# Attention in which the scores are made once, and transposed after the exponential

## The chip, the core and the metric

The kernel runs on one core of a Trainium2 chip. TensorE (PE in the rows; PEld is its weight load) multiplies matrices into the eight PSUM banks of 512 float32 columns; VectorE (DVE), ScalarE (ACT) and GpSimd (POOL) do the rest, and SyncE (SP) issues the large transfers. Each engine takes its own list of instructions in order, and they wait for one another by semaphores. The metric is the time of the program on the device in microseconds (us), median of several runs.

## The reference

One decoder layer over 1024 tokens of width 1024. The part that matters here is the attention of 8 query heads in 2 key/value groups (head size 64), with three branches whose outputs are weighed by gates:

```python
s_c = einsum(q, k_cmp) - slope * d_c;  p_c = masked_softmax(s_c, d_c >= 0)      # 63 compressed keys
s_s = einsum(q, ks) - slope * d_s;     p_s = masked_softmax(s_s, d_s >= 0)      # selected blocks
s_w = einsum(q, kw) - slope * d_w;     p_w = masked_softmax(s_w, window of 512) # sliding window
o   = g0 * p_c @ v_cmp + g1 * p_s @ vs + g2 * p_w @ vw
```

With 16 blocks and a top-k of 16 the selected branch sees every earlier key, so it is plain causal attention over 1024 tokens. Around the attention stand a projection (23 units of 128 columns), a convolution branch, an output projection and a gated feed-forward of width 2816.

## The kernel before

Everything is laid out with channels on the partitions. A float32 operand of a matmul is split into a high and a low part, and products are made of two or three of these parts. The large products (`unit_tile`, L309 to L319) run in 97 units; they are not touched.

The attention stands between unit 22 and unit 23 and is a loop over the two groups `g`. In each group the query tiles `i` are 0 to 7 (128 queries of each of 4 heads), and key tiles `j` are of 128 keys. Per group it goes in these stages:

1. Copies and splits of keys and queries (ScalarE L520 to L548, VectorE L718 to L743), and the compressed keys (PE L964, L973).
2. The first scores, queries on the partitions: 32 rows (head, query tile), each of two units of up to two PSUM banks. PE makes them (`scores`, L982 and L983, masks L996), VectorE takes the negated maximum of each branch (L747) into `nmax`. PE may be two rows ahead.
3. `nmax` is turned on PE (L1033), split (L552, L764) and taken by two DMAs into rows of the query operand `QB`; the values are turned too (L1040, L555, L766).
4. The second scores, keys on the partitions, in 74 steps (`STEPS`, one key tile of one branch of one query tile, 4 heads side by side in 512 columns). The maximum comes in through the extra rows of `QB` and `KB`, so that the exponential can be taken directly: PE L1059, L1060 and a mask L1063; ScalarE takes the exponential twice from PSUM, rounded (L565, into `PTH`) and in full (L566, into `EB`); VectorE subtracts (L799, into `PTL`); PE multiplies by the values (L1078 to L1080). The scores of step s+3 are made ahead of the values of step s, in four PSUM banks.
5. At the end of each query tile the three outputs `OT` are copied from PSUM (VectorE L805 twice, ScalarE L572 once), turned on PE (L1089), divided and weighed on VectorE (L780, L784, L791), summed on POOL (L440, L442), and squared on ScalarE (L576).

The order of all this is written out by hand; the waits say how far one engine may be ahead of another.

## Time and profile before

| | us |
|---|---|
| Three runs | 1532.84, 1532.97, 1534.7 |
| Span of the profiled execution | 1532.4 |
| PE busy | 1453.2 |
| DVE busy | 707.4 |
| ACT busy | 457.7 |
| Attention, 297 to 673 us of the span | 376 |

The profiled execution is told by its span alone; the runs' median lies 0.6 us above it. In the page a busy time is the time in which at least one instruction of the engine was under way, and "mean ns of one" the duration of one, which for matmuls and ScalarE instructions overlaps with the next one. The distance from start to start of two instructions in the timeline is what one of them costs in a row of them.

### The profile page before, as it was taken

How to read it: one execution, taken by the hardware profiler on the slowest of the kernel's cores; microseconds unless marked ns; L12 is line 12 of the kernel's file. 1: busy time of each engine (PE TensorE's matmuls, PEld its weight loads, DVE VectorE, ACT ScalarE, POOL GpSimd, SP SyncE). 2: the span in 40 equal slices, each digit the busy share in tenths (PEclk: the TensorE clock that was granted, in tenths of full speed). 3: DMA queues.
4: the chain of work that ended last, by engine and by line, in shares of the span. 5: the costliest groups of instructions: out<-in, count | busy, mean ns of one | idle time of the engine just before them, and what ended most of it. 6: DMA issues, size and time to landing. Idle time of an engine off the chain costs nothing.

```text
span 1532.4 us, 17433 instructions
## 1 busy us (share of the span) xinstructions
PE 1453.2 (95%) x6670; PEld 1153.6 (75%) x6670; DVE 707.4 (46%) x871; ACT 457.7 (30%) x638; POOL 62.5 (4%) x56
## 2 busy tenths in 40 slices
PE   3999999999898998989989999999999999999995
PEld 2888888876565765668868888888888888888874
DVE  6422331186565866654353434343443524344356
ACT  5221222323677236842123211212111121211211
POOL 1100000000211002110020000000000000000000
PEclk9999999799998999999989999999999999999997
DMA  5211111000000030011101111111111011111102
GB/s 185 68 41 41 55 55 68 8 1 3 1 1 7 1 112 1 1 56 55 55 14 55 44 53 41 55 55 41 55 41 55 32 64 41 55 41 41 55 1 109
DMA packets 18690, 67.65 MB, mean 44 GB/s; under 512 B 2088, under 2 KB 2856, under 8 KB 18472
## 3 DMA queue, kind: packets, MB, share of 16 engines
q1 hardware_dynamic: 18396, 66.03, 12.2%
q0 software_dynamic: 240, 0.93, 0.3%
q8 instruction: 31, 0.51, 0.1%
q14 instruction: 23, 0.19, 0.0%
HBM read 63.01 MB, written 4.19 MB: 44 GB/s over the span
## 4 chain that ended last, share of the span: by engine, by line
PE 88%; DVE 5%; issue 2%; ACT 2%; POOL 1%; DMA 1%; DVEq 0%; SPq 0%; ACTq 0%; POOLq 0%
PE PS L314 18%; PE PS L315 18%; PE PS L318 18%; PE PS L1156 5%; PE PS L1160 5%; PE PS L1157 5%; PE PS L982 3%; PE PS L983 2%; PE PS L1078 2%; PE PS L1079 2%; PE PS L1080 2%; PE PS L1059 1%; PE PS L1060 1%; DVE nmax L747 1%; PE PS L964 1%
## 5 line engine op out<-in xcount | busy, mean ns | idle before, releaser
L314 PE MATMUL PS<-R,wh 128*128 128x512 f32 x1200 | 471.1, 393 | 9.5 <-DVE R L285 7.6
L315 PE MATMUL PS<-R,wh 128*128 128x512 f32 x1200 | 470.0, 392 | 0.0
L318 PE MATMUL PS<-R,wl 128*128 128x512 f32 x1200 | 371.8, 391 | 0.0
L314 PEld LDWEIGHTS PS<-R,wh 128*128 128x128 f32 x1200 | 227.3, 189 | 59.9 <-issue 12.6
L315 PEld LDWEIGHTS PS<-R,wh 128*128 128x128 f32 x1200 | 227.2, 189 | 47.5 <-issue 0.2
L318 PEld LDWEIGHTS PS<-R,wl 128*128 128x128 f32 x1200 | 227.1, 189 | 47.4
L299 ACT ACTIVATE wh<-raw 128x1024 fp32r<-128x1024 f32 x97 | 101.7, 1049 | 176.5 <-PE PS L1160 174.0
L882 DVE TENSOR_TENSOR F<-PS,F 128x1024 f32<-128x1024 f32 x88 | 107.6, 1223 | 92.1 <-PE PS L1160 92.1
L306 DVE TENSOR_TENSOR wl<-raw,wh 128x1024 fp32r<-128x1024 f32 x97 | 120.0, 1245 | 62.9 <-ACT wh L299 62.2
L1156 PE MATMUL PS<-R,wh 128*128 128x512 f32 x352 | 137.1, 389 | 1.1 <-DVE wl L306 1.1
L1157 PE MATMUL PS<-R,wh 128*128 128x512 f32 x352 | 136.9, 389 | 0.0
L799 DVE TENSOR_TENSOR wl<-raw,wh 128x512 fp32r<-128x512 f32 x148 | 102.7, 696 | 61.3 <-ACT raw L566 59.4
L862 DVE SCALAR_TENSOR_TENSOR F<-PS,params,F 128x1023 f32<-128x1023 f32 x22 | 28.2, 1283 | 180.6 <-ACT F L617 180.6
L1160 PE MATMUL PS<-R,wl 128*128 128x512 f32 x352 | 108.4, 389 | 0.0
L747 DVE TENSOR_REDUCE nmax<-PS 128x1 f32<-128x64 f32 (+4 forms) x192 | 91.3, 537 | 16.7 <-PE PS L996 15.7
L565 ACT ACTIVATE wh<-PS 128x512 fp32r<-128x512 f32 x148 | 91.4, 617 | 21.0 <-PE PS L1063 12.5
L566 ACT ACTIVATE raw<-PS 128x512 f32<-128x512 f32 x148 | 91.9, 621 | 0.0
L982 PE MATMUL PS<-R 128*128 128x512 f32 (+4 forms) x208 | 86.6, 417 | 2.6 <-DVE R L742 1.8
L617 ACT ACTIVATE F<-PS,params 128x1024 f32<-128x1024 f32 x22 | 26.6, 1208 | 192.5 <-PE PS L318 192.5
L1078 PE MATMUL PS<-wh,R 128*65 128x512 f32 x148 | 68.1, 460 | 12.6 <-DVE wl L799 6.0
L870 DVE TENSOR_TENSOR F<-F,PS 128x1024 f32<-128x1024 f32 x22 | 26.9, 1221 | 115.0 <-PE PS L318 114.9
L983 PE MATMUL PS<-R 74*128 74x512 f32 (+4 forms) x208 | 79.0, 386 | 0.0
(138 smaller groups left out, 1376.2 us busy)
## 6 DMA issues: line engine op xcount, KB each, us to landing
raw<-in_w_units SPq DMA_DIRECT2D x97, 512.0 KB, 3.2
F<-in_xT SPq DMA_DIRECT2D x16, 512.0 KB, 7.5
outT<-F SPq DMA_DIRECT2D x8, 512.0 KB, 3.0
F<-in_w_cmp SPq DMA_DIRECT2D x1, 2048.0 KB, 7.7
masks<-in_masks POOLq DMA_DIRECT2D x1, 448.0 KB, 5.6
R<-in_alibi_q POOLq DMA_DIRECT2D x2, 160.0 KB, 5.3
R<-R SPq DMA_DIRECT2D x4, 48.0 KB
R<-in_alibi_k POOLq DMA_DIRECT2D x1, 136.0 KB, 3.4
```

The source lines that it names most:

```text
L306: nc.vector.tensor_tensor(wl[:, slot, :], raw[:, slot, :], f32(wh[:, slot, :]), ALU.subtract)\
L314: nc.tensor.matmul(out, w_h, hi(kt)[:, cols], start=first, stop=False)
L315: nc.tensor.matmul(out, w_h, lo(kt)[:, cols], start=False, stop=False)
L318: last = nc.tensor.matmul(out, w_l, hi(kt)[:, cols], start=False, stop=end)
L747: return nc.vector.tensor_reduce(nmax[:, br, i, h:h + 1], pair(2 * (b % 2) + unit)[:, col:col + count], AX.X, ALU.max, negate=True)
L799: nc.vector.tensor_tensor(PTL[s % 4], EB[s % 4], f32(PTH[s % 4]), ALU.subtract).then_inc(pt_lo, 1)
L882: nc.vector.tensor_tensor(x1, pair(DOWN_PAIRS[d]), x1, ALU.add).then_inc(down_added, 1)
L982: nc.tensor.matmul(out, QA[:, i, h, :], KA[:, key:key + count], start=True, stop=False)
L983: nc.tensor.matmul(out, QB[0:DH + AR, i, h, :], KB[0:DH + AR, key:key + count], start=False, stop=not masked)
L1156: nc.tensor.matmul(out, w_h, act_at(par_pair, a, 0)[:, cols], start=a == 0, stop=False)
L1157: nc.tensor.matmul(out, w_h, act_at(par_pair, a, 1)[:, cols], start=False, stop=False)
L1160: last = nc.tensor.matmul(out, w_l, act_at(par_pair, a, 0)[:, cols], start=False, stop=a == 1)
```

## The change

The two kinds of scores become one. A phase is now (group, query tile, part), part 0 for the selected branch and part 1 for the window, 32 phases in all; the compressed branch is attached to one of the two parts (`CMP_IN_A`). A phase has four rows, one for each head, and its steps are the key tiles of its branches, 148 over both groups.

For a row PE makes the scores with queries on the partitions, VectorE takes the maximum, and ScalarE takes the exponential with the maximum as bias into SBUF (`EA`, `EB`). For a step PE turns four 128x128 blocks of these exponentials (`turn_weights`) into one PSUM bank, ScalarE copies them rounded into `PTH`, VectorE subtracts from PSUM into `PTL`, and PE multiplies by the values two steps later. The rows of a phase are put among the steps of the phase before it (`step_of_row`). The row scores, the turned outputs and the turned values share two pairs of PSUM banks (`SLOTS`). All the `OT` copies are now ScalarE's. The compressed keys and values of both groups are made ahead of the loop. The DMAs of the maxima are gone. SyncE loads units 24 to 26 before the attention, and the residual input x after it.

```diff
+PHASES = [(g, i, part) for g in range(KV) for i in range(TT) for part in range(2)]
+STEPS = [(p, i, br, j) for p, (g, i, part) in enumerate(PHASES) for br, j in key_tiles(i, part)]
+def step_of_row(r):
+    p, h = divmod(r, GROUP)
+    if p == 0:
+        return -1
+    if p == len(PHASES) // KV:
+        return FIRST_STEP[p] - 1
+    return FIRST_STEP[p - 1] + h * (FIRST_STEP[p] - FIRST_STEP[p - 1]) // GROUP
+ROWS_AT = [[r for r in range(NROWS) if step_of_row(r) == s] for s in range(-1, len(STEPS))]
...
@@ sync
-                for part, src, done in ((0, MH, mt_hi), (1, ML, mt_lo)):
-                    sp.dma_start(f32(QB[row:row + 3, :, :, :])..., f32(src[0:96, :])).then_inc(m_in, 16)
...
+            sp.wait_ge(t_ready, KV * NS)
+            sp.wait_ge(pt_lo, KV * NS)
+            for k in range(KT):
+                sp.dma_start(F1[:, X1 + k, :], xT[k]).then_inc(x1_in, 16)
@@ scalar
-                        act.wait_ge(st_ready, NS * g + s + 1)
-                        nc.scalar.activation(PTH[s % 4], PS[:, s % 4, :], ACT.Exp).then_inc(pt_hi, 1)
-                        nc.scalar.activation(EB[s % 4], PS[:, s % 4, :], ACT.Exp).then_inc(e_ready, 1)
+            def exponentials(r):
+                act.wait_ge(max_ready, r + 1)
+                last = nc.scalar.activation(weights[:, 0:wide], scores[:, 0:wide], ACT.Exp, bias=nmax[:, r, 0:1])
+                if with_cmp:
+                    last = nc.scalar.activation(weights[:, wide:wide + CW], scores[:, wide:wide + CW], ACT.Exp,
+                                                bias=nmax[:, r, 1:2])
+                last.then_inc(e_ready, 1)
...
+            for s in range(KV * NS + 2):
+                    act.wait_ge(t_ready, s + 1)
+                    if s > 3:
+                        act.wait_ge(pv_done, s - 3)
+                    nc.scalar.activation(PTH[s % 4][0:tall, :], PS[0:tall, 4 + s % 2, :], ACT.Copy).then_inc(pt_hi, 1)
+                    ...
+                        nc.scalar.activation(OT[STEPS[ENDS[b] - 1][2]], PS[0:DH + 1, 6 + b % 2, :], ACT.Copy)
+                    for r in ROWS_AT[s + 1]:
+                        exponentials(r)
+                    ...
@@ vector
+            for s in range(KV * NS + 1):
+                    dve.wait_ge(pt_hi, s + 1)
+                    nc.vector.tensor_tensor(PTL[s % 4][0:tall, :], PS[0:tall, 4 + s % 2, :], f32(PTH[s % 4][0:tall, :]),
+                                            ALU.subtract).then_inc(pt_lo, 1)
+                    ...
+                for t in range(TURNS):
+                    if step_of_turn(t) == s:
+                        weigh(t)
+                    for r in ROWS_AT[s + 1]:
+                        maxima(r)
@@ tensor
-                    for c in range(0, width, BANK):
-                        scores(bank + c // BANK, 0, h, i, key + c, min(BANK, KEYS - key - c), ...)
-                def key_scores(s):
-                    ...
+                for c in range(0, wide, BANK):
+                    scores(c, key + c, min(BANK, wide - c), c == 0 and diag >= BANK and not edge)
+            def turn_weights(s):
+                if s == FIRST_STEP[p]:
+                    pe.wait_ge(e_ready, GROUP * (p + 1))
+                if s > 1:
+                    pe.wait_ge(pt_lo, s - 1)
+                for h in range(GROUP):
+                    last = nc.tensor.transpose(PS[0:tall, 4 + s % 2, h * P:(h + 1) * P],
+                                               weights_of(h, part)[:, col:col + tall], ident)
+                last.then_inc(t_ready, 1)
...
+            for s in range(KV * NS):
+                turn_weights(s)
+                ...
+                for r in ROWS_AT[s + 1]:
+                    row_scores(r)
+                ...
+                    for v in values_at(s):
+                        values(v)
             order = [4, 5, 6, 7, 0, 1, 2, 3]
-            for n in (OUT0, OUT0 + 1):
-                unit_matmuls(pe, n, 0, 0, 0, n % 3, m_hi, m_lo, order, order[:4])
+            unit_matmuls(pe, OUT0, 0, 0, 0, OUT0 % 3, m_hi, m_lo, order, order[:4])
+            turn(TURNS - 1)
+            pe.wait_ge(o_scaled, TURNS)
+            unit_matmuls(pe, OUT0 + 1, 0, 0, 0, (OUT0 + 1) % 3, m_hi, m_lo, order, order[:4])
```

On ScalarE, in the steps of a group of the kernel before: L565 and L566 are the two exponentials of a step, L576 the squares.

```order
L565 ACTIVATE wh<-PS 128x512 [waits pv_done,st_ready]
L566 ACTIVATE raw<-PS 128x512
L562 REGISTER_ALU
L565 ACTIVATE wh<-PS 128x512 [waits pv_done,st_ready]
L566 ACTIVATE raw<-PS 128x512
L575 REGISTER_ALU
```

ScalarE in the changed kernel, in the phase of query tile 6, window part: L632 is the copy into `PTH`, L650 the copy of an output, L611 the exponential of a row of the next phase.

```order
L632 ACTIVATE wh<-PS 128x512 [waits pv_done,t_ready]
L650 ACTIVATE PBm<-PS 65x512 [waits ot_turned,pv_done]
L611 ACTIVATE F1<-PS,nmax 128x896 [waits max_ready]
L613 ACTIVATE F1<-PS,nmax 128x64
L632 ACTIVATE wh<-PS 128x512 [waits pv_done,t_ready]
L611 ACTIVATE F1<-PS,nmax 128x896 [waits max_ready]
L613 ACTIVATE F1<-PS,nmax 128x64
L632 ACTIVATE wh<-PS 128x512 [waits pv_done,t_ready]
```

Before, each ScalarE instruction of a step waited for PE alone. Now a copy, which VectorE waits for, stands behind an exponential, which itself waits for VectorE.

VectorE before, in the steps: L799 is the subtraction, L805 a copy of an output.

```order
L805 COPY PBm<-PS 65x512 [waits pv_done]
L798 REGISTER_ALU
L799 TENSOR_TENSOR wl<-raw,wh 128x512 [waits e_ready]
L798 REGISTER_ALU
L799 TENSOR_TENSOR wl<-raw,wh 128x512 [waits e_ready]
L780 RECIPROCAL coef<-PS 128x12 [waits ot_turned]
```

VectorE in the changed kernel: L882 is the subtraction, L850 and L852 the maxima of a row of the next phase.

```order
L882 TENSOR_TENSOR wl<-PS,wh 128x512 [waits pt_hi]
L850 TENSOR_REDUCE nmax<-PS 128x1 [waits s_ready]
L852 TENSOR_REDUCE nmax<-PS 128x1
L882 TENSOR_TENSOR wl<-PS,wh 128x512 [waits pt_hi]
L850 TENSOR_REDUCE nmax<-PS 128x1 [waits s_ready]
L852 TENSOR_REDUCE nmax<-PS 128x1
```

The maxima, which had a stage of their own in which VectorE did little else, now stand each behind the subtraction of a step.

PE in the changed kernel, in a window phase: L1143 turns exponentials, L1111, L1112 and L1118 make a row, L1156 to L1158 multiply by the values.

```order
L1143 MATMUL PS<-consts,F 128x128 [waits pt_lo]
L1143 MATMUL PS<-consts,F 128x128 x3
L1111 MATMUL PS<-R 128x512 [waits e_ready]
L1112 MATMUL PS<-R 128x512
L1111 MATMUL PS<-R 128x128
L1112 MATMUL PS<-R 128x128
L1111 MATMUL PS<-R 128x64
L1112 MATMUL PS<-R 128x64
L1118 MATMUL PS<-masks 128x128 x2
L1118 MATMUL PS<-masks 128x64
L1156 MATMUL PS<-wh,R 65x512 [waits pt_lo]
L1157 MATMUL PS<-wh,R 65x512
```

A row waits for the exponential of the row two before it, so PE can be ahead of the other two by a step, not more.

## Rows read from the trace of the kernel before

**Rows 1.** The page: span, busy us (share) xinstructions, GB/s in 40 slices.
```profile
span 1532.4 us, 17433 instructions
PE 1453.2 (95%) x6670; PEld 1153.6 (75%) x6670; DVE 707.4 (46%) x871; ACT 457.7 (30%) x638; POOL 62.5 (4%) x56
...
GB/s 185 68 41 41 55 55 68 8 1 3 1 1 7 1 112 1 1 56 55 55 14 55 44 53 41 55 55 41 55 41 55 32 64 41 55 41 41 55 1 109
```

**Rows 2.** Windows: length, busy us of PE, PEld, DVE, ACT, POOL; PE clock, DMA.
```profile
297.00:307.00 10.00, 8.71 (x41) 8.36 (x41) 5.39 (x8) 2.49 (x5) 0.00 (x0) 0.50 0.00 0
307.00:363.00 56.00, 55.60 (x325) 41.91 (x326) 47.94 (x100) 8.94 (x9) 0.00 (x0) 0.96 0.00 1
...
561.00:673.00 112.00, 103.11 (x496) 65.11 (x497) 68.58 (x114) 82.92 (x173) 16.95 (x15) 0.99 0.12 45
sum 376.00, PE 346.19 PEld 239.85 DVE 250.09 ACT 200.27 POOL 35.50; mean PE 43.27 PEld 29.98 DVE 31.26 ACT 25.03 POOL 4.44
```

**Rows 3.** Timeline of the steps: start, us, engine, line, operation.
```profile
428.87 0.65 ACT L566 ACTIVATE raw<-PS 128x512 f32<-128x512 f32 x1
429.34 0.66 ACT L565 ACTIVATE wh<-PS 128x512 fp32r<-128x512 f32 x1
429.55 0.69 DVE L799 TENSOR_TENSOR wl<-raw,wh 128x512 fp32r<-128x512 f32 x1 [0.28 <-ACT raw L566]
```

**Rows 4.** Groups by form, DVE, 280 to 760 us: busy us, mean ns, idle before.
```profile
L799 DVE TENSOR_TENSOR wl<-raw,wh 128x512 fp32r<-128x512 f32 x148 | 102.7, 696 | 61.3 <-ACT raw L566 59.4
L747 DVE TENSOR_REDUCE nmax<-PS 128x1 f32<-128x640 f32 x40 | 31.9, 813 | 0.0
L791 DVE TENSOR_TENSOR F<-PS,coef 128x768 f32<-128x768 f32 x16 | 15.2, 949 | 0.1
L747 DVE TENSOR_REDUCE nmax<-PS 128x1 f32<-128x64 f32 x64 | 14.0, 219 | 16.6 <-PE PS L996 15.7
L732 DVE SCALAR_TENSOR_TENSOR R<-F,R 64x512 fp32r<-64x512 f32 x16 | 10.8, 683 | 0.3
L747 DVE TENSOR_REDUCE nmax<-PS 128x1 f32<-128x1024 f32 x8 | 9.7, 1213 | 0.0
L747 DVE TENSOR_REDUCE nmax<-PS 128x1 f32<-128x128 f32 x16 | 3.8, 278 | 0.0
```

**Rows 5.** Groups by form, ACT, 280 to 760 us.
```profile
L565 ACT ACTIVATE wh<-PS 128x512 fp32r<-128x512 f32 x148 | 91.4, 617 | 21.0 <-PE PS L1063 12.5 <-PE PS L1060 7.9
L576 ACT ACTIVATE F<-F 128x256 f32 x14 | 5.8, 418 | 32.7 <-POOL F L442 32.7
L590 ACT ACTIVATE R<-PS,params 128x1024 fp32r<-128x1024 f32 x4 | 4.3, 1113 | 12.2 <-PE PS L1117 12.2
L526 ACT ACTIVATE hidc<-PS,posb 128x63 f32<-128x63 f32 x4 | 1.3, 314 | 12.1 <-PE PS L964 12.1
```

**Rows 6.** Timeline of PE: the gates' transposes, and two score matmuls in a row.
```profile
286.80 1.03 PE L942 MATMUL PS<-consts,F 128*128 128x128 f32 x8
320.23 0.40 PE L983 MATMUL PS<-R 74*128 74x512 f32 x1
320.47 0.40 PE L982 MATMUL PS<-R 128*128 128x512 f32 x1
```

**Rows 7.** Windows of 1 us inside the steps of the first group.
```profile
392.00:393.00 1.00, 0.48 (x2) 0.33 (x3) 0.86 (x3) 1.00 (x3) 0.00 (x0) 1.00 0.00 0
399.00:400.00 1.00, 0.00 (x0) 0.00 (x0) 0.03 (x1) 1.00 (x3) 0.00 (x0) 1.00 0.00 0
401.00:402.00 1.00, 1.00 (x4) 0.71 (x3) 0.84 (x2) 1.00 (x3) 0.00 (x0) 0.50 0.00 0
```

**Rows 8.** Timeline: ScalarE's first copy for the attention; the ends of the attention.
```profile
289.73 1.06 ACT L520 ACTIVATE raw<-F 64x1024 f32 x1
...
668.57 0.39 PE L1080 MATMUL PS<-wl,R 128*65 128x512 f32 x1
...
684.86 0.46 PE PS L318 x2
```

More of the change, by code:

```diff
@@ new lines, in values_turned @@
+                    .then_inc(v_hi, 1)
+            act.wait_ge(qkv_ready, N_QKV)
+            for g in range(KV):
+                to_compress(CK[:, g, :], g, 0, ck_ready)
+            for half in range(2):
+                keys(0, half)
+            for g in range(KV):
+                to_compress(CV[g], g, 1, cv_ready)
+            act.wait_ge(hidk_ready, 1)
+            act.wait_ge(posb_ready, 1)
+            nc.scalar.activation(hidc[:, 0:2, :], PS[:, 6, 0:2 * NCMP].rearrange("p (g n) -> p g n", g=KV),
+                                 ACT.Gelu_apprx_tanh, bias=posb[:, 0:1]).then_inc(geluk_ready, 1)
@@ L809, in _ @@
-                steps.leave()
+            for half in range(2):
+                keys(0, half)
+            dve.wait_ge(kcp_ready, 1)
+            nc.vector.tensor_copy(kcmp[:, :, :], PS[0:DH, 7, 0:2 * NCMP].rearrange("p (g n) -> p g n", g=KV))\
+                .then_inc(kcmp_ready, 1)
+            dve.wait_ge(vcp_ready, 1)
+            nc.vector.tensor_copy(vcmp[:, :, :], PS[0:NCMP, 6, 2 * P:2 * P + KV * DH].rearrange("p (g d) -> p g d", g=KV))\
+                .then_inc(vcmp_ready, 1)
+            for h in range(GROUP):
+                queries(0, 0, h)
@@ new lines, in _, with maxima @@
+            keys_compressed(0)
+            values_turned(0)
+            def maxima(r):
+                p, h = divmod(r, GROUP)
+                g, i, part = PHASES[p]
+                dve.wait_ge(s_ready, r + 1)
+                scores = pair(slot("row", r))
+                wide = P * (i + 1 if part == 0 else min(i, WT) + 1)
+                with_cmp = CMP_IN_A[i] == (part == 0)
+                last = nc.vector.tensor_reduce(nmax[:, r, 0:1], scores[:, 0:wide], AX.X, ALU.max, negate=True)
+                if with_cmp:
+                    last = nc.vector.tensor_reduce(nmax[:, r, 1:2], scores[:, wide:wide + CW], AX.X, ALU.max, negate=True)
+                last.then_inc(max_ready, 1)
@@ new lines, in _ @@
+            last.then_inc(vt_ready, 1)
+            for g in range(KV):
+                pe.wait_ge(cv_ready, 2 * g + 2)
+                for l in range(CMP_BLOCK // 2):
+                    last = nc.tensor.matmul(PS[:, 4 + g, 0:NCMP], W1C[:, 1, l, :],
+                                            CV[g][:, 2 * l:2 * l + CMP_STRIDE * (NCMP - 1) + 1:CMP_STRIDE],
+                                            start=l == 0, stop=l == CMP_BLOCK // 2 - 1)
+                last.then_inc(hidv_ready, 1)
+            pe.wait_ge(geluk_ready, 1)
@@ new lines, in _ @@
+            pe.wait_ge(posb_ready, 1)
+            nc.tensor.matmul(PS[0:DH, 7, 0:KV * NCMP], w2c[:, 0, :], hidc[:, 0:2, :].rearrange("p g n -> p (g n)"),
+                             start=True, stop=True).then_inc(kcp_ready, 1)
+            pe.wait_ge(geluv_ready, 2)
+            for g in range(KV):
+                last = nc.tensor.matmul(PS[0:NCMP, 6, 2 * P + g * DH:2 * P + (g + 1) * DH], hidc[:, 2 + g, :], w2c[:, 1, :],
+                                        start=True, stop=True)
+            last.then_inc(vcp_ready, 1)
@@ new lines, in values @@
+            def values(s):
+                p, i, br, j = STEPS[s]
+                tall = CW if br == CMP else P
+                pe.wait_ge(pt_lo, s + 1)
+                first, end = s == 0 or s in ENDS, s + 1 in ENDS
+                b = sum(e <= s for e in ENDS)
+                if first and b > 1:
+                    pe.wait_ge(ot_copied, b - 1)
+                n, out = (0, TT, 2 * TT)[br] + j, PS[0:DH + 1, 6 + b % 2, :]
+                nc.tensor.matmul(out, VH[0:tall, n, 0:DH + 1], PTH[s % 4][0:tall, :], start=first, stop=False)
+                nc.tensor.matmul(out, VL[0:tall, n, 0:DH + 1], PTH[s % 4][0:tall, :], start=False, stop=False)
+                nc.tensor.matmul(out, VH[0:tall, n, 0:DH + 1], PTL[s % 4][0:tall, :], start=False, stop=end).then_inc(pv_done, 1)
```

606 lines of the change are left out of this document (291 added, 315 removed).

## Prediction

> **What bounds the kernel now.** I read the page first: PE is busy 95% of a span of 1532.4 us, no other engine half of it [rows 1]. So an edit that only takes work from PE ought to pay. Then the windows, to find the attention: it lies between 297 and 673 us, 376 us, of which PE is busy 346; the first scores of a group take 56 us, its steps 112, and the rest is preparation [rows 2]. Third the timeline in the steps: ScalarE starts an exponential every 0.47 us, though each is told as 0.65, and VectorE starts 0.03 us after the second of them ends, 428.87 + 0.65 = 429.52 against 429.55 [rows 3]. That is what a hand-over between two engines costs there. Last the groups by form, for the price of every operation that the change keeps in another order [rows 4, 5]. What I look for is whether PE stays the bound when the other two engines are made to wait for each other.
>
> **What PE gets rid of.** Two score matmuls of 512 columns start 0.24 us apart [rows 6]. The second scores, 148 x 2 of these and 56 masks, go: about 352 x 0.235 = 83 us less. The first scores lose the columns beyond the diagonal, which every row of a 512-bank carried: some 20 us. Four transposes for each of 148 steps come: eight take 1.03 us [rows 6], of which the last one's tail is 0.27 (one alone is a 128-column matmul), so 0.11 to 0.13 each, 592 of them 65 to 77 us. That price was seen at the full clock; it is the nearest row to the new ones, which read the same float32 form from SBUF. In the new loop PE's own work is transposes 68, values 148 x 3 x 0.235 = 104, rows 84 and their masks 17, turned outputs 14: about 285 us. The maxima's DMAs and their waits go too, and one set-up of the second group.
>
> **What the new order makes ScalarE and VectorE do.** In each of 103 of the 148 steps at least one row of the next phase is worked on (88 with one, 12 with two, 3 with four; one more set of four comes ahead of the first step). In such a step the order rows show a closed round: ScalarE's copy; VectorE's subtraction, which waits for it; VectorE's maximum, queued behind the subtraction; ScalarE's exponential, which waits for the maximum; and the next step's copy, queued behind the exponential. Nothing in this round can overlap with the rest, however far ahead PE is. Its pieces:
>
> - Copy 0.60 (between the 0.617 mean and the undisturbed ones) and subtraction 0.69 [rows 4, 5]; three hand-overs of 0.03 to 0.05 [rows 3]; off it go 0.12 that a ScalarE instruction starts ahead of the other's told end, and 0.06 for VectorE's: 1.23 us, x 103 = 126.7 us. That the subtraction now reads PSUM where it read SBUF is not in a row of that size; between nothing more and 0.1 us each (10 us), I take nothing, since the 768-column L791 reads PSUM in 0.949, which is 0.69 scaled up.
> - The maxima: they have the very lengths of before, 128 wide ones and 64 of 64 columns. From 0.278 at 128 over 0.813 at 640 to 1.213 at 1024, 0.16 for a small one that follows [rows 4]: 98 us without the first phase.
> - The exponentials with a bias: the nearest rows with a per-partition operand from PSUM are 0.314 at 63 columns and 1.113 at 1024 [rows 5], a straight line of 0.26 + 0.00083 per column. 128 wide ones with 67,584 columns in all give 89, the 64 small ones 0.19 each 12: 100 us without the first phase. Without the bias' share it would be 90, and by L565's own rate of 0.617 for 512 some 95.
> - Where a step has two or four rows, maximum and exponential of neighbours do overlap: 12 us off.
>
> Together 313 us. To it come, on the same path: 45 steps without a row at VectorE's pace of 0.65 (29 us); 15 times the weighing, three dependent VectorE instructions of which the largest is 0.949, 1.5 us in all, and the squares at 0.45 of ScalarE, in the same queues (29 us); 12 splits of queries at 0.683, less their overlap, and the keys of the second group (12 us); 14 starts of phases of up to four steps, where the transposes must wait for the exponential just made, 0.5 us each (7 us). That is 390 us. The last phase, which has no rows and runs at PE's 1.16 us a step, adds 3; the change of group, where the last values are multiplied, copied, and the new values split before a maximum may start, 5; the output copies of ScalarE, which wait for values queued on PE behind two rows, 4. The loop then is 402 us, against PE's 285 in it: PE stands still for 30% of it, and no longer sets the time.
>
> **Before and after the loop.** ScalarE is free at 289.7, and its copies of 1024 columns take 1.06 us each [rows 8]. It has four of compressed keys, two of keys, four of compressed values: 300.3. PE, at half its clock there as before (0.50, rows 2), needs until about 312.5 for three sets of 16 matmuls; the queries (eight of 0.53), the values' high part (about 1.1) and the exponential's table follow, then the first four rows and transposes. I put the first copy of step 0 at 322.5, between 319 and 324. The last value matmul then is at 322.5 + 402 = 724.5, where it was at 668.6 [rows 8]: 56 us later. At the end half of unit 23 now covers the output copy, but unit 24 waits on PE for the last weighing and for VectorE's split, which stands behind the norm's first instructions; before, both halves covered these, up to 684.9 [rows 8]. I count 3 us against the change. The 4 MB of x come after the loop, on SyncE's queue ahead of unit 27; x is first needed some 29 us after the last values, and unit 27 later. At the rate of the kernel's start (185 GB/s, rows 1: 22 us) that is hidden; if it were not, some 5 us.
>
> Sum: 1532.4 + 56 + 3 = 1591.4, and with the 0.6 us between this span and the runs' median 1592.
>
> **A rule against the change.** In the first group's steps PE was busy 48% of a microsecond and kept the clock of 1.00, but after two in which it stood still the clock was 0.50, the lower of its two levels, 1.2 GHz [rows 7]. So short gaps did no harm there, a gap of 2 us did.
>
> The Trainium skill (TensorE: Matmul & The Clock Gate, section "A second HAM failure mode: psum-queue depth-cycling") tells of a kernel that cycles through PSUM banks, whose small pauses made the clock go up and down and cost throughput. By that rule the time is that of the first rival below; the trace agrees only for the longer gap.
>
> **Rivals.**
>
> 1. *The clock falls in the loop.* PE would idle some 0.5 to 1 us in each round and 2 us at starts of phases and at the change of group. At the lower clock PE's 285 us become about 525 (matmuls double, weight loads and waits don't), more than the 402 of the round, and PE sets the pace: +120 us if it were so throughout. At that pace PE is busy all the time and the clock comes back, so a third of the loop is what I would expect: +43, 1635 us. For it: the gaps. Against it: the 1.00 at 48% [rows 7]. 16%.
>
> 2. *PE stays the bound, and the change pays.* If ScalarE and VectorE do not form the round, because maxima and exponentials find room in the time in which PE multiplies, the loop takes PE's 285 us and some 10 for starts: it ends at about 618 instead of 669, less the 3 at the end: 1484 us. It decides where a step with a row takes less than PE's 1.16 + 0.8 = 2 us; the round has 1.23 + 0.81 + 0.79 = 2.8 already for 640 columns. Idle of VectorE in the steps before, 61 us behind L566 [rows 4], speaks for it: there is room on the engine, if the order let it be used. 9%.
>
>    The Trainium skill (TensorE: Matmul & The Clock Gate, section "Architectural detail: the array is 16× 32×32, not 1× 128×128") says that ScalarE and VectorE are strict FIFO while PE may pull weight loads ahead. By it the round stands, and no rival of this kind is left; the trace of before has no instruction that shows it by itself.
>
> 3. *It comes out even.* The round is shorter than counted by a sixth (exponentials at the rate without bias, ScalarE's overlap twice as large, starts hidden) and the prologue shorter: 402 + 25 becomes 345 + 22: within a few us of 1532. 4%.
>
> **How the numbers follow.** Forecast 71%, rival 1 16%, rival 2 9%, rival 3 4%. The prices in the round are off by perhaps 5% either way (16 us), the overlaps at the starts by 10; the errors that I can name (PSUM reads, PE not ahead after a turned output, cold starts) all make it longer. The forecast's own range is 1565 to 1625; with rival 1 in it the range is 1560 to 1645, and rival 2 is left out. What is within 0.2% (3 us) can't be told from no change here. Faster: rival 2 and half of rival 3, 0.11. Same: 0.01. Slower: 0.88.
>
> **What would show it.** In the changed kernel the waits should have ScalarE's exponentials waiting for VectorE's maxima, and VectorE's subtraction waiting for ScalarE's copy, each some 60 to 150 us in all, and the chain of waits should lead through these two engines in the loop, with PE busy for some 85% of the longer span instead of 95%. A step of query tile 7's rows (1024 columns) should last 3.5 us from copy to copy, one of 640 columns 2.7 to 2.8. PE should be busy 70 to 75% between 323 and 725 us, with the clock near 1.00; 0.7 there would be rival 1. Groups L747's time should be unchanged. I am wrong if a step with a row takes about 2 us (the round is not closed), if the transposes cost twice the 0.13 us (PE back as the bound, +70 on its side), or if the feed-forward after the attention changes its length, which nothing here touches.

## The result, and the profile after

| | before | after |
|---|---|---|
| median us (lowest to highest) | 1533.63 (1532.84 to 1534.7) | 1637.07 (1636.52 to 1638.9) |
| span of the profiled execution | 1532.4 | 1634.8 |
| mean granted clock of the span | 0.969 | 0.926 |
| end of the last value matmul (start: 668.57 and 768.96) | 669 | 769.4 |

After over before is 1.068 [1.0664, 1.0695]: 103 us slower. It is slower, as forecast, and within the range, but only in the part of it that the first rival had added: the forecast's own range ended at 1625. The forecast of 1592 was 45 us short, and the time is the one that the first rival had given (1635).

The page of the changed kernel, against [rows 1]: span, busy times, then the row of clocks and the chain of waits.

```profile
span 1634.8 us, 17328 instructions
...
PE 1484.8 (91%) x6970; PEld 1196.5 (73%) x6970; DVE 691.1 (42%) x839; ACT 499.8 (31%) x723; POOL 50.1 (3%) x56
...
PEclk9999999756989767999997999999999999999997
...
PE 78%; DVE 11%; ACT 6%; issue 4%; DMA 0%; POOL 0%; DVEq 0%; SPq 0%; ACTq 0%
```

Each digit of the clock row is 41 us, and the loop is the ninth to the nineteenth. Six of these are below 9, and five of the six (5 and 6, then 7, 6 and 7) lie at the starts of the two groups. In the chain VectorE and ScalarE together hold 17% of the span, 278 us.

Its waits between 320 and 790 us (who waited for whom: us in all, times, longest):

```profile
DVE wl L882 <- ACT wh L632: 205.0, 127, 4.5
ACT F L611 <- DVE nmax L852: 67.6, 41, 2.8
ACT F L611 <- DVE nmax L850: 65.8, 44, 2.9
ACT PBm L650 <- PE PS L1158: 56.4, 36, 4.9
...
PE PS L1143 <- ACT F L613: 36.4, 16, 4.0
...
ACT wh L632 <- PE PS L1143: 30.5, 45, 1.4
```

The first three rows are the closed round: VectorE's subtraction waits for ScalarE's copy, ScalarE's exponentials wait for VectorE's maxima. It is visible link by link in the timeline of the two engines at query tile 7 (start, us, engine, line):

```profile
503.31 0.59 ACT L632 ACTIVATE wh<-PS 128x512 fp32r<-128x512 f32 x1
...
503.93 0.69 DVE L882 TENSOR_TENSOR wl<-PS,wh 128x512 fp32r<-128x512 f32 x1 [1.67 <-ACT wh L632]
504.54 1.22 DVE L850 TENSOR_REDUCE nmax<-PS 128x1 f32<-128x1024 f32 x1
...
505.79 1.11 ACT L611 ACTIVATE F<-PS,nmax 128x1024 f32<-128x1024 f32 x1 [1.42 <-DVE nmax L850]
506.80 0.59 ACT L632 ACTIVATE wh<-PS 128x512 fp32r<-128x512 f32 x1
...
507.43 0.69 DVE L882 TENSOR_TENSOR wl<-PS,wh 128x512 fp32r<-128x512 f32 x1 [1.67 <-ACT wh L632]
508.03 1.22 DVE L850 TENSOR_REDUCE nmax<-PS 128x1 f32<-128x1024 f32 x1
509.28 1.11 ACT L611 ACTIVATE F<-PS,nmax 128x1024 f32<-128x1024 f32 x1 [1.89 <-DVE nmax L850]
510.30 0.59 ACT L632 ACTIVATE wh<-PS 128x512 fp32r<-128x512 f32 x1
```

Each instruction starts within 0.04 us of the told end of the one before it or ahead of it, and the next copies start at 506.80 and 510.30: 3.5 us from copy to copy, as forecast. The 24 steps with one row of 640 columns and no compressed part, forecast at 2.7 to 2.8 us, took 2.77 at the least, but 3.34 in the median. What was not priced shows in windows: length, then busy us of PE, PEld, DVE, ACT, POOL, the clock, DMA. First the whole loop, then its four quarters, then three single windows.

```profile
325.00:770.00 445.00, 357.63 (x1949) 262.71 (x1948) 222.39 (x400) 225.77 (x445) 22.38 (x31) 0.80 0.01 1
325.00:436.00 111.00, 89.01 (x441) 65.06 (x440) 49.10 (x101) 52.64 (x112) 5.81 (x8) 0.69 0.00 1
436.00:551.00 115.00, 91.35 (x537) 66.93 (x535) 65.69 (x104) 64.30 (x118) 4.93 (x7) 0.91 0.01 2
551.00:661.00 110.00, 87.51 (x446) 65.03 (x445) 49.32 (x103) 51.43 (x113) 6.63 (x10) 0.69 0.00 1
661.00:770.00 109.00, 89.77 (x533) 65.68 (x532) 58.27 (x92) 57.40 (x105) 5.01 (x7) 0.92 0.01 2
...
325.00:335.00 10.00, 7.61 (x44) 7.16 (x43) 4.25 (x12) 5.66 (x14) 0.00 (x0) 0.50 0.00 0
...
385.00:395.00 10.00, 9.53 (x32) 5.81 (x31) 4.08 (x7) 4.41 (x10) 0.00 (x0) 0.50 0.00 0
...
497.00:507.00 10.00, 8.62 (x48) 5.53 (x46) 5.35 (x7) 6.03 (x11) 0.00 (x0) 1.00 0.00 0
```

The clock was 0.80 over the loop and 0.69 in the first half of either group. At 385 to 395 us it was 0.50, the lower level (1.2 GHz), and PE was busy 9.53 of 10 us there: at that clock PE is the bound again, while VectorE and ScalarE are busy less than half the time. In the timeline of that place, all three engines (start, us, engine, line):

```profile
380.35 0.69 DVE L882 TENSOR_TENSOR wl<-PS,wh 128x512 fp32r<-128x512 f32 x1 [2.45 <-ACT wh L632]
...
382.41 0.63 PE L1158 MATMUL PS<-wl,R 128*65 128x512 f32 x1
...
382.84 1.05 PE L1143 MATMUL PS<-consts,F 128*128 128x128 f32 x4
...
383.08 0.59 ACT L650 ACTIVATE PBm<-PS 65x512 f32<-65x512 f32 x1 [2.76 <-PE PS L1158]
383.57 1.25 ACT L611 ACTIVATE F<-PS,nmax 128x512 f32<-128x512 f32 x2
...
384.71 0.59 ACT L632 ACTIVATE wh<-PS 128x512 fp32r<-128x512 f32 x1
...
385.33 0.69 DVE L882 TENSOR_TENSOR wl<-PS,wh 128x512 fp32r<-128x512 f32 x1 [2.85 <-ACT wh L632]
```

A 512-column matmul takes 0.42 to 0.44 us from start to start here (0.24 in [rows 6], at the full clock), the four transposes 1.05 (0.60 to 0.66 at the full clock). And the copy of an output (L650) has waited 2.76 us for PE, with both exponentials and the next copy queued behind it: at a low clock the round passes through PE as well. The step takes 5.0 us, from one subtraction to the next (380.35 to 385.33).

Where the excess lies is told best by the phases, each from its first copy to the next phase's. In us, group 0 (phase 2i is the selected part of query tile i, 2i+1 its window part; phases 0 to 6, of short rows, are called the narrow ones below, 7 to 14 the wide ones). The middle column was summed after the result, from the prediction's prices:

| phases | by the prediction's prices, step by step | after |
|---|---|---|
| 0 to 6 | 65 | 81.2 |
| 7 to 14 | 123 | 126.6 |
| 15 with the change of group | 15.5 | 19.9 |

Group 1 reads 82.2, 125.6 and 8.4 (its last phase has no rows). The wide phases were priced within 3%; the narrow ones, at the low clock, were short by 16 to 17 us in each group.

### The profile page after: what moved, and what is told of

The parts are those of the page before. It is cut to its first block, busy times and chain, and to the rows that moved or that the text cites. A ratio compares the mean times of both kernels' runs of the same rounds, so it can differ in the third digit from the quotient of the medians.

```text
span 1634.8 us, 17328 instructions
## 1 busy us (share of the span) xinstructions
PE 1484.8 (91%) x6970; PEld 1196.5 (73%) x6970; DVE 691.1 (42%) x839; ACT 499.8 (31%) x723; POOL 50.1 (3%) x56
## 4 chain that ended last, share of the span: by engine, by line
PE 78%; DVE 11%; ACT 6%; issue 4%; DMA 0%; POOL 0%; DVEq 0%; SPq 0%; ACTq 0%
PE PS L364 17%; PE PS L365 17%; PE PS L368 17%; PE PS L1247 5%; PE PS L1251 5%; PE PS L1248 5%; DVE wl L882 4%; DVE nmax L850 3%; PE PS L1143 3%; ACT wh L632 2%; PE PS L1111 2%; PE PS L1112 2%; ACT F L611 2%; PE PS L1156 1%; PE PS L1157 1%
## 5 line engine op out<-in xcount | busy, mean ns | idle before, releaser
L882 DVE TENSOR_TENSOR wl<-PS,wh 128x512 fp32r<-128x512 f32 (+1 forms) x148 | 101.0, 689 | 205.1 <-ACT wh L632 205.0
L1143 PE MATMUL PS<-consts,F 128*128 128x128 f32 (+1 forms) x592 | 110.0, 317 | 67.1 <-ACT F L613 36.4
L1143 PEld LDWEIGHTS PS<-consts,F 128*128 128x128 f32 (+1 forms) x592 | 82.0, 160 | 117.0 <-ACT F L613 43.8
L611 ACT ACTIVATE F<-PS,nmax 128x640 f32<-128x640 f32 (+7 forms) x128 | 88.9, 698 | 133.9 <-DVE nmax L852 67.6
L1111 PE MATMUL PS<-R 128*128 128x512 f32 (+4 forms) x256 | 103.6, 408 | 27.8 <-ACT F L613 9.1
L632 ACT ACTIVATE wh<-PS 128x512 fp32r<-128x512 f32 (+1 forms) x148 | 86.4, 593 | 30.7 <-PE PS L1143 30.5
L850 DVE TENSOR_REDUCE nmax<-PS 128x1 f32<-128x640 f32 (+7 forms) x128 | 89.5, 700 | 14.6 <-PE PS L1118 13.9
L1111 PEld LDWEIGHTS PS<-R 128*128 128x128 f32 x256 | 62.5, 244 | 38.8 <-ACT F L613 12.1
L1112 PE MATMUL PS<-R 74*128 74x512 f32 (+4 forms) x256 | 88.7, 389 | 0.0
```

The source lines that it names most:

```text
L611: last = nc.scalar.activation(weights[:, 0:wide], scores[:, 0:wide], ACT.Exp, bias=nmax[:, r, 0:1])
L850: last = nc.vector.tensor_reduce(nmax[:, r, 0:1], scores[:, 0:wide], AX.X, ALU.max, negate=True)
L882: nc.vector.tensor_tensor(PTL[s % 4][0:tall, :], PS[0:tall, 4 + s % 2, :], f32(PTH[s % 4][0:tall, :]), ALU.subtract).then_inc(pt_lo, 1)
L1111: nc.tensor.matmul(out, QA[:, i, h, :], KA[:, key:key + count], start=col % BANK == 0, stop=False)
L1112: return nc.tensor.matmul(out, QB[0:DH + AR, i, h, :], KB[0:DH + AR, key:key + count], start=False, stop=stop)
L1143: last = nc.tensor.transpose(PS[0:tall, 4 + s % 2, h * P:(h + 1) * P], weights_of(h, part)[:, col:col + tall], ident)
```

## The experiments

Ratios are against the kernel before, run on the same chip (medians there 1534.91, 1532.04, 1533.9 and 1531.22 for the four sets). "Loop" is the time from 325 us to the last value matmul of the profiled execution, 444 in the changed kernel. The expectations weigh three explanations of its length: the closed round, PE's low clock, and from set two on the queue in which ScalarE's output copies stand.

Set one asks whether the round is closed, and whether PE's amount of work matters.

**e1: VectorE takes the maxima of the coming rows ahead of the subtraction.** The round's second and third link are exchanged, so that a maximum no longer waits for ScalarE's copy; the weighing of a turned output moves with them.

```diff
             for s in range(KV * NS + 1):
                 if s < KV * NS:
+                    ... (weigh, if due)
+                    for r in ROWS_AT[s + 1]:
+                        maxima(r)
                     dve.wait_ge(pt_hi, s + 1)
                     nc.vector.tensor_tensor(PTL[s % 4] ...
-                    for r in ROWS_AT[s + 1]:
-                        maxima(r)
```

> Edit: VectorE takes the maxima of a step's rows (and weighs a turned output) before the subtraction of that step instead of behind it; everything else is the changed kernel's. Round theory (copy, subtraction, maximum, exponential, next copy each wait for the one before): the maximum no longer stands behind the subtraction, so the round is cut to copy and exponential on ScalarE beside maximum and subtraction on VectorE, about 1.3 to 1.5 us for a row of 640 columns instead of 2.8. PE's 2.0 us a step then sets the pace, the clock stays at its higher level, the loop falls from 444 us to 300 to 340 and the time to 1495 to 1535 us. Clock theory alone (the round is not what makes PE wait): PE's work and its pauses are what they were, 1620 us or more.

Measured: 1541.67 us (1540.46 to 1545.37), ratio 1.0053 [1.0032, 1.0073]; loop 350 us. In the page the subtraction's group, whose last numbers are the idle time before it, and the window of the whole loop:

```profile
L889 DVE TENSOR_TENSOR wl<-PS,wh 128x512 fp32r<-128x512 f32 (+1 forms) x148 | 101.0, 683 | 33.9 <-ACT wh L632 33.6
```

```profile
325.00:676.00 351.00, 312.50 (x1950) 233.78 (x1949) 222.95 (x400) 223.63 (x445) 22.41 (x31) 0.90 0.01 2
```

That is 7 us above the 1495 to 1535 expected of the round and far from the 1620 of the clock alone. The wait for the copy fell from 205 to 34 us, and 95 of the 103 us are back with not one operation removed: VectorE and ScalarE are as busy as before the exchange (222 and 226 against 223 and 224). That is the closed round, shown. The clock rose with it, from 0.80 to 0.90, and has a share in the 95; e2 and e6 below tell the two apart. Phases 7 to 14 went from 126.6 to 95.8 us and phases 0 to 6 from 81.2 to 63.9.

**e2: ScalarE's exponentials of a step stand behind the next step's copy** (except in a phase's last step). The same round, opened on the other engine.

```diff
                     nc.scalar.activation(PTH[s % 4][0:tall, :], PS[0:tall, 4 + s % 2, :], ACT.Copy)...
+                    for r in (ROWS_AT[s] if s and exp_late(s - 1) else []):
+                        exponentials(r)
...
-                    for r in ROWS_AT[s + 1]:
+                    for r in ([] if exp_late(s) else ROWS_AT[s + 1]):
                         exponentials(r)
```

> Edit: ScalarE takes the exponentials of a step's rows behind the copy of the next step instead of ahead of it, except at the last step of a phase, where the next transposes need them. VectorE's order is the changed kernel's. Round theory: the other place at which the round can be opened; inside a phase a step costs the longer of ScalarE's 1.3 and VectorE's 1.5 us for 640 columns, so PE sets the pace there, but the last step of each of 30 phases still goes the whole round. Between e1 and the changed kernel: 1510 to 1560 us. Clock theory alone: 1620 us or more.

Measured: 1577.17 (1572.07 to 1577.77), ratio 1.0277 [1.026, 1.0294]; loop 379 at a clock of 0.87. It takes back 60 us, less than the expected least. In the wide phases it is nearly as good as e1 (98.7 us for phases 7 to 14); the narrow ones take 74.4 (63.9 in e1), at a clock of 0.72 (0.79). ScalarE's copies now wait 90.7 us for PE's transposes (30.5 before), but 28.0 of these lie in phases 7 to 14 of group 0 and only 15.4 in its phases 0 to 6: the wait shows PE setting the pace in the wide phases, and what holds the narrow ones is not separated.

**e3: every transpose of the exponentials is made twice**, 592 more of them.

```diff
-                for h in range(GROUP):
+                for h in list(range(GROUP)) * 2:
```

> Edit: every transpose of exponentials is made twice (592 more on PE, the same result written over itself). Clock theory: PE waits in the loop and its clock falls to 1.2 GHz for part of it; 68 us more of PE work fill the pauses, the clock stays high, and the loop comes down from 444 towards the round's 402: 1595 to 1615 us with more work, mean granted clock of the span from 0.93 to 0.97 or more. If the clock is only a symptom and the round's length is the 444 us: no change, 1637 to 1645. If PE is the bound: 68 us more, 1690 or above.

Measured: 1643.1 (1641.01 to 1644.46), ratio 1.0706 [1.0686, 1.0726]; loop 449, its clock 0.91. The granted clock rose as the clock theory said, from 0.80, and the time did not fall. The narrow phases of group 0 did (81.2 to 76.6), those of group 1 did not (82.2 to 82.7), and the wide ones got longer (126.6 to 128.7, and 125.6 to 129.6 in group 1). Where a copy waits for the transposes, as at the start of a phase, whose first set must wait for the exponential just made, they are on the round itself: in the wide phases of group 0 the copies waited 12.5 us for them, 5.3 in the changed kernel. The time is the one expected if the clock were only a symptom (1637 to 1645); e6 shows that this branch is wrong as well. The price of a transpose can be read here (busy, mean):

```profile
L1143 PE MATMUL PS<-consts,F 128*128 128x128 f32 (+1 forms) x1184 | 170.5, 291 | 51.8 <-ACT F L613 30.3
```

Against 110.0 us for 592 in the changed kernel, 592 more cost 60.5 us busy, 0.10 each. That difference mixes two clocks, but at the full clock alone it is the same: the next matmul starts 0.79 us after the first of eight transposes (489.73 to 490.52 us).

**e4: one of the three value products is left out**, 148 of 444 matmuls.

```diff
-                nc.tensor.matmul(out, VL[0:tall, n, 0:DH + 1], PTH[s % 4][0:tall, :], start=False, stop=False)
```

> Edit: the product of the low part of the values with the high part of the weights is left out (148 of 444 value matmuls; the output loses some precision). Round theory: PE is not the bound at the higher clock, nothing is won beyond 10 us; clock theory adds that PE does still less, so its clock is lower for longer and the time the same or up to 15 us longer: 1625 to 1650 us. If PE's amount of work were the bound of the loop: 148 x 0.235 = 35 us less at the higher clock, more at the lower: 1590 to 1602 us.

Measured: 1626.43 (1624.12 to 1628.51), ratio 1.0592 [1.0572, 1.0611]; loop 436, its clock 0.78. 148 matmuls are 35 us of PE at the full clock and more at the lower one; 11 came back, in the profiled execution 8, and of these 7 in the narrow phases (77.4 against 81.2 in group 0, 79.2 against 82.2 in group 1). In phases 7 to 14 of group 0 taking PE's work away did nothing: 126.6 and 126.6. PE's amount of work isn't the bound there. That its speed doesn't matter isn't shown, since the clock of these phases was lower too, 0.87 against 0.90.

Set two moves ScalarE's output copies, and gives PE something to do in its pauses.

**e5: output copies behind the step's exponentials.**

```diff
-                    if s < KV * NS and ENDS[b] - 1 in values_at(s):
+                    if s == NS - 1 and ENDS[b] - 1 in values_at(s):
...
                     for r in ROWS_AT[s + 1]:
                         exponentials(r)
+                for b in range(3 * TURNS):
+                    if s < KV * NS and s != NS - 1 and ENDS[b] - 1 in values_at(s):
+                        ... (the same copy)
```

> Edit: ScalarE copies the outputs of a branch behind the exponentials of the same step instead of ahead of them. The loop's 42 us beyond the round lie in the phases of query tiles 0 to 3 (about 16 us a group) and at the change of group. Queue theory: there a step has two or four rows, PE makes all of them before the values that the output copy waits for, and ScalarE's exponentials stand behind that copy (56 us of wait in front of the output copies). With the copy behind them the loop gets 15 to 30 us shorter: 1607 to 1622 us. Clock theory: the excess is PE at 1.2 GHz, the copies only show it: 1630 us or more.

Measured: 1633.06 (1631.98 to 1635.24), ratio 1.0654 [1.0627, 1.0681]: 4 us less, which is not the 1607 to 1622 of the queue theory but the clock theory's 1630 or more. Group 0 says why. Phases 0 to 6 gained 6 us (75.2, at a clock of 0.70 against 0.63); phases 7 to 14 lost 4 (130.4), since the copy had stood in ScalarE's wait for a maximum and cost nothing, and now stands between exponential and copy, on the round.

**e6: six constant matmuls of 512 columns fill PE's pause at the start of each phase**, ahead of the wait for the exponentials. Their result is overwritten by the transposes.

```diff
+                if s > 1:
+                    pe.wait_ge(pt_lo, s - 1)
+                if s == FIRST_STEP[p] and p:
+                    for _ in range(6):
+                        nc.tensor.matmul(PS[:, 4 + s % 2, :], masks[:, M_ID:M_ID + P], masks[:, 0:BANK], start=True, stop=True)
                 if s == FIRST_STEP[p]:
                     pe.wait_ge(e_ready, GROUP * (p + 1))
-                if s > 1:
-                    pe.wait_ge(pt_lo, s - 1)
```

The wait for the subtraction that frees the bank moves ahead of the six; the transposes still wait for both.

> Edit: at the first step of each phase but the first, PE makes six matmuls of 512 columns of a constant, into the bank that the transposes then overwrite, before it waits for the last exponential of the phase. PE stands still there for 2 us or more, so at the higher clock they cost nothing. Clock theory: the pauses that let the clock fall are filled, the first halves of the groups run at 0.9 instead of 0.69, and 15 to 25 us come back: 1612 to 1622 us. Queue theory: the clock is not what makes the early phases long: within 5 us of 1637, or some us more, since at the lower clock the six take 2.6 us.

Measured: 1610.82 (1609.3 to 1613.43), ratio 1.0515 [1.0486, 1.0544]; loop 417. Its four quarters in windows, against those of the changed kernel above:

```profile
325.00:742.00 417.00, 348.27 (x2105) 240.26 (x2130) 220.69 (x400) 224.01 (x443) 22.43 (x31) 0.95 0.01 1
325.00:429.00 104.00, 85.53 (x512) 58.84 (x519) 50.95 (x105) 54.46 (x115) 5.84 (x8) 0.91 0.00 1
429.00:534.00 105.00, 86.86 (x532) 59.64 (x538) 62.21 (x98) 60.94 (x112) 4.93 (x7) 1.00 0.01 2
534.00:638.00 104.00, 84.72 (x500) 58.12 (x506) 49.58 (x106) 52.13 (x115) 6.56 (x10) 0.89 0.00 1
638.00:742.00 104.00, 91.15 (x566) 63.65 (x570) 57.94 (x92) 56.48 (x103) 5.10 (x7) 1.00 0.00 1
```

186 more matmuls, every other instruction in the same order, and 26 us less. The edit takes no work and no wait away, so what is left to give the time is the clock, and the windows show it rise, 0.69 to 0.91 and 0.89 in the first halves of the groups. PE was busy for less time (348 us against 358) with more to do. So of the 42 us by which the loop was longer than forecast, some 26 are the clock's. They lie in the narrow phases (81.2 to 73.3 us in group 0, 82.2 to 75.2 in group 1) and in the wide ones alike (126.6 to 120.3, 125.6 to 119.4). In the wide ones the step with a row of 640 columns now has a median of 2.78 us, the forecast's 2.7 to 2.8, where it was 3.34.

This run also tells the round from the clock: in phases 7 to 14 of group 0 the clock is 1.00 both here and in e2, and the closed round takes 120.3 us, the opened one 98.7.

**e7: e1 and e2 together.**

> Edit: e1 (maxima ahead of the subtraction) and e2 (exponentials behind the next step's copy) together. In e1 VectorE already waits 84 us for PE's rows and the ScalarE queue holds copy and exponential of one step; inside a phase e2 adds nothing that PE could use. If the round alone was the matter: 1530 to 1545 us, as e1. If ScalarE's order still costs PE something inside the phases: 1510 to 1530.

Measured: 1561.01 (1556.56 to 1571.8), ratio 1.02 [1.0148, 1.0252], some 20 us slower than e1 alone and outside both expected ranges. The maxima now wait 116.7 us for PE's rows (83.1 in e1) and ScalarE's copies 91.1 for its transposes. A row waits for the exponential of the row two before it, so exponentials that come later would make rows later; that reading fits the waits, but no run separates it from the clock, which was 0.88 in this loop and 0.90 in e1's. It stays open.

**e8: e1 and e5 together.**

> Edit: e1 (maxima ahead of the subtraction) with e5 (output copies behind the exponentials). Queue theory: what e5 wins in the early phases is won here too, less than there since the round is open: 1520 to 1532 us, which would be at or just below the kernel before. Clock theory: as e1, 1540 us.

Measured: 1520.49 (1520.34 to 1523.35), ratio 0.9921 [0.9897, 0.9946]. This version beats both kernels: it is 12 us faster than the kernel before, as the queue theory had it. Its loop and the loop's first quarter in windows:

```profile
325.00:655.00 330.00, 300.57 (x1944) 226.32 (x1944) 223.30 (x400) 222.26 (x443) 22.40 (x31) 0.94 0.01 1
325.00:407.00 82.00, 72.85 (x493) 55.72 (x492) 55.09 (x111) 57.71 (x124) 5.83 (x8) 0.94 0.00 1
```

The same move that gave 4 us in e5 gives 21 here, and nearly all of it in the narrow phases: phases 0 to 6 take 53.4 us (63.9 in e1), phases 7 to 14 94.7 (95.8). With the round open the moved copies no longer lengthen the wide phases, as they did in e5. But the clock of phases 0 to 6 rose as well, from 0.79 in e1 to 0.91, and no run tells how much of the 21 is the queue's and how much the clock's.

Sets three and four try the fill on top, and the copies in the narrow phases alone.

**e9: e8 with three filling matmuls per phase** (as in e6, `range(3)`).

> Edit: e8 (maxima ahead of the subtraction, output copies behind the exponentials) with three of e6's constant matmuls ahead of each phase. In e8 the loop's clock is 0.89 to 0.95 in three quarters of it and PE still waits some 25 us for the exponentials at starts of phases. If the clock theory holds there too, another 5 to 10 us come: 1510 to 1516 us. If the open round left no pause long enough to matter, the 9 us of added matmuls (31 x 3 x 0.215 = 20 us, half of it in pauses) cost 0 to 10: 1520 to 1530.

Measured in five runs: 1524.13 (1523.62 to 1524.78), ratio 0.9937 [0.9923, 0.995]. Nothing on e8's 0.9921 [0.9897, 0.9946]. The loop's clock went from 0.94 to 0.96 only, and not everywhere up: in phases 0 to 6 of group 0 it was 0.85 against 0.91 (55.5 us against 53.4), and in those of group 1 higher (55.0 us against 57.6). Three matmuls instead of six may be part of it; six were not tried here.

**e10: e5 and e6 together.**

> Edit: e5 (output copies behind the exponentials) and e6 (six constant matmuls ahead of each phase) together, in the changed kernel with its closed round. With the clock up and the queue of output copies gone, the loop should be what the sum of the round gave, 402 us against 444, and the time 1592 to 1602 us. If the round itself was counted too short, it stays at e6's 1611.

Measured: 1627.08 (1626.12 to 1627.84), ratio 1.061 [1.0593, 1.0626]: 16 us slower than e6 alone and outside both expectations, at nearly the same clock (0.93 in the loop against 0.95). Phases 7 to 14 take 127.1 us in group 0 and 124.9 in group 1, 120.3 and 119.4 in e6: the moved copies are on the round, as in e5.

**e11: e6, with output copies moved only in steps that have two or more rows.** **e12: the same selective move on e1.** In both the condition is

```diff
+                    if s < KV * NS and s != NS - 1 and len(ROWS_AT[s + 1]) > 1 and ENDS[b] - 1 in values_at(s):
```

> Edit: e6 (six constant matmuls ahead of each phase), and the output copies behind the exponentials only in steps with two or more rows; in the others they stay ahead, as in the changed kernel, where the wait for VectorE's maximum hides them. In e5 the phases with such steps won about 6 us a group, while the later phases lost 4, an output copy being added to the round there. If that reading holds, e6's 1611 becomes 1597 to 1604 us, and the loop is within 5 us of the 402 that was summed. If e10's 1627 came from something else than the late copies, it stays at 1611 or above.

> Edit: e1 (maxima ahead of the subtraction) with the output copies behind the exponentials only in steps with two or more rows. With the round open PE sets the pace in the late phases, so where the copy stands there should matter little: as e8, 1517 to 1524 us. If e8 owes its 21 us on e1 to the late phases too, this one lies between them, 1528 to 1535 us.

Measured: e11 1608.5 (1608.23 to 1611.47), ratio 1.0495 [1.0471, 1.0518]; e12 1521.95 (1520.91 to 1522.62), ratio 0.993 [0.9907, 0.9952]. e12 is e8's equal, so with the round open all of the gain lies in the narrow phases, as expected. e11 is e6 within the intervals and not the 1597 to 1604 expected. Its phases 7 to 14 take 120.4 and 119.4 us, as in e6, which confirms that it was the late copies that cost e10 its 12 us there. That it gains nothing, while e12's copies gain 20 on e1, is not explained: the wait in front of the output copies fell from 28 us to 11, and phases 0 to 6 took 74.4 and 73.5 us against 73.3 and 75.2; the clock of these phases in group 0 was 0.80 against 0.87.

## Why the forecast had the direction and not the size

Step by step, as the prediction put them:

- *What PE gets rid of and what it takes on.* Right. A set of four transposes takes 0.60 to 0.66 us at the full clock with its tail, and 0.10 each by e3, against 0.11 to 0.13 priced. PE's work in the loop was priced at 285 us; in e8, where the round is open, it is busy 300.6 at a clock of 0.94. Over the whole span PE is busy 1429.1 us in e8 against 1453.2 [rows 1], and the last value matmul ends 13.5 us earlier than in the kernel before (655.5 against 669.0): PE did get lighter.
- *The closed round, 313 us.* Right, shown by e1, and at equal clocks by e2 against e6. Its prices held. From the groups by form between 285 and 800 us (busy, mean), against [rows 4, 5]:

```profile
L850 DVE TENSOR_REDUCE nmax<-PS 128x1 f32<-128x640 f32 x40 | 32.7, 818 | 3.1 <-PE PS L1118 2.6
```

```profile
L632 ACT ACTIVATE wh<-PS 128x512 fp32r<-128x512 f32 x132 | 77.3, 594 | 30.1 <-PE PS L1143 30.0
L611 ACT ACTIVATE F<-PS,nmax 128x640 f32<-128x640 f32 x40 | 31.7, 792 | 62.8 <-DVE nmax L850 35.6 <-DVE nmax L852 27.3
...
L611 ACT ACTIVATE F<-PS,nmax 128x1024 f32<-128x1024 f32 x8 | 8.9, 1114 | 11.0 <-DVE nmax L850 11.0
...
L611 ACT ACTIVATE F<-PS,nmax 128x128 f32<-128x128 f32 x16 | 5.9, 367 | 9.7 <-DVE nmax L852 5.4 <-DVE nmax L850 4.3
```

  The straight line of 0.26 + 0.00083 per column gave 0.79, 1.11 and 0.37. The subtraction that now reads PSUM takes 0.689 us, against 0.696 from SBUF: nothing more was the right choice. The maxima of 640 columns read 818 ns against 813.
- *The wait of the subtraction, 60 to 150 us.* Too low; it is 205.0. In the round VectorE stands still while ScalarE makes the exponential and the next copy, 1.67 us at 1024 columns; 103 such gaps of 1.2 to 1.7 us are 150 alone, and the narrow phases at the low clock have gaps of up to 4.5. The wait of the exponentials, 67.6 + 65.8 = 133 us, was inside.
- *The loop of 402 us, with the clock near 1.00.* This is the step that failed: the clock stood in the sum at its full level, as if the pauses cost nothing. The clock was 0.80 and the loop 444 us. The prediction leaned on 1.00 at 48% busy in one microsecond [rows 7], in steps in which PE stood still for 9 of 109 us (376 to 485 us, clock 0.98). In phases 0 to 6 of the changed kernel it stood still for 18 of 81 us, in pauses of up to 2.2 us, and got 0.50 for whole stretches (325 to 345, 385 to 395 us). e6 shows that some 26 of the 42 us are this. By the phases (81.2 and 82.2 against 65 twice), the clock's share and the under-priced narrow steps together are 33 us; the other places are the change of group (4 us more) and 3 us in the wide phases of each group. That the wide phases came so near is in part luck: at the clock of 1.00 in e6 they take 120.3 us, 3 less than priced, and the low clock added 6.
- *Rival 1.* Its time came, its mechanism in half of its form, and that its time fits to 2 us is luck: its +43 was a third of its upper bound, while e6 puts some 26 us on the clock and leaves 15 open. It had PE setting the pace for about a third of the loop. Single windows with PE busy 9.5 of 10 us show that; but other windows of 0.50 have PE busy 7.6 of 10, so that low clock and round add up there instead of one replacing the other. Its statement that weight loads don't double is so, but they do grow: one of 128 float32 columns is told as 0.190 us at the full clock and 0.333 at the lower. Its factor of 525/285 = 1.84 for all of PE's work is near what rows show (0.43 against 0.24 for a matmul of 512 columns, 1.05 against 0.60 to 0.66 for a set of transposes). The Trainium skill (TensorE: Matmul & The Clock Gate, section "A second HAM failure mode: psum-queue depth-cycling") describes such a clock that goes up and down over small pauses; this trace agrees, with 0.50, 0.84 and 0.50 in the three windows of 10 us from 335 to 365.
- *PE busy 70 to 75% in the loop, 85% of the span.* It is 80% and 91%, for the same reason: the same work at a lower clock is longer work. A busy share near its old value was no sign of health. The chain of waits did lead through VectorE and ScalarE, but PE still held 78% of it over the span.
- *The output copies, 4 us.* With the round closed, moving them is worth 4 (e5); with it open, 21 (e8), a share of the clock in it. A price of a wait holds for one arrangement of the others only.
- *First copy at 322.5, tail +3.* 325.4, above the 319 to 324 given, and +2 (the end lies 865.4 us behind the last value matmul, 863.4 before).
- *Rivals 2 and 3.* Not this kernel. Rival 2's PE-bound loop of about 295 us is not reached by e8 either (330 at a clock of 0.94), but e8 goes most of the way from 444, by order alone.

Open: 15 us of the loop in e6 (417 against 402 at a clock of 0.95). By the phases, those 0 to 6 are 18 us over their price (73.3 and 75.2 against 65 twice) and the change of group 5, while the wide ones are 6 under. In phases 0 to 6 four or two rows can stand in one step, and the prediction let their maxima and exponentials overlap. The timeline of the first set of four has (ScalarE, start, us):

```profile
320.99 0.37 ACT L611 ACTIVATE F<-PS,nmax 128x128 f32<-128x128 f32 x1 [0.19 <-DVE nmax L850]
322.06 0.37 ACT L611 ACTIVATE F<-PS,nmax 128x128 f32<-128x128 f32 x1 [0.70 <-DVE nmax L850]
322.66 0.37 ACT L611 ACTIVATE F<-PS,nmax 128x128 f32<-128x128 f32 x1 [0.23 <-DVE nmax L850]
323.73 0.37 ACT L611 ACTIVATE F<-PS,nmax 128x128 f32<-128x128 f32 x1 [0.70 <-DVE nmax L850]
```

1.07 us and 0.60 by turns: with two pairs of banks, PE's row is a third link every second time. No run separates this from the clock, which was still 0.87 and 0.86 there.

## What to carry to other kernels

Before engines are made to hand work to each other in both directions, write down the order of each queue and follow one item round: if the path comes back to its own start, the sum of that path is the time, whatever the busy shares say. One exchange of two instructions in a queue was worth 95 us here, what it gave back to the clock included, so look for the order that opens the round before judging the algorithm. And once a round makes TensorE pause in every step, read the clock as a term of the sum with its own range, not as a rival beside it.

## What the hardware showed that was not expected

- More work on PE made the kernel faster: 186 matmuls on constants, placed only where PE waited anyway, took the loop from 444 to 417 us and its clock from 0.80 to 0.95 (e6). The same idea in a place that others wait for (e3) raised the clock to 0.91 and gained nothing, and with three matmuls where the loop's clock was 0.94 already (e9) it gained nothing either.
- A third of the value products, 35 us of PE at the full clock, was worth 11 us (e4). The loop's clock was 0.78 against 0.80 in the two profiled executions; over all runs it was 0.919 to 0.926 of the span against 0.924 to 0.926, too near to say that less work lowered it.
- A busy share does not tell the clock: 10 us with PE busy 8.62 had 1.00, 10 us with PE busy 9.53 had 0.50.
